# First loads reordered, two units sharing a norm's high parts, the reciprocal ahead of the splits, and two more buffers for the last weights

## The reference

```python
h = rmsnorm(x, g[0]);  y = even_mixer(h)      # gated heads (HGRN2) and retention, h @ w_in, then @ w_out
x = x + rmsnorm(y, g[1])
h = rmsnorm(x, g[2]);  x = x + rmsnorm(square(relu(h @ w1)) @ w2, g[3])      # MLP 0
h = rmsnorm(x, g[0']); x = x + rmsnorm(odd_mixer(h), g[1'])                  # mLSTM heads, causal conv
h = rmsnorm(x, g[2']); x = x + rmsnorm(square(relu(h @ w1')) @ w2', g[3'])   # MLP 1
h = rmsnorm(x, n) * (1 + scale) + shift       # shift, scale, gate = silu(c) @ w_ada + b_ada
y_attn = (attention(h) * silu(g_attn)) @ w_o_attn;  y_conv = (short_conv(h) * silu(g_conv)) @ w_o_conv
x = x + gate * ((sigmoid(m_attn) * y_attn + sigmoid(m_conv) * y_conv) @ w_out)
return rmsnorm(x, final_g)
```

## Time and profile before

| | us |
|---|---|
| median of 3 executions | 1048.25 (1048.1 to 1050.12) |
| profiled execution | 1048.74 |
| its span | 1046.7 |
| TensorE busy | 998.1 (95%) |
| VectorE busy | 669.5 (64%) |
| ScalarE busy | 510.9 (49%) |
| mean granted clock of TensorE | 0.982 of full |

### The profile page before, as it was taken

The page is one execution under the profiler, slowest core; times in us unless marked ns, Lnnn a source line. Parts: engine busy times, 40 slices in busy tenths (PEclk is TensorE's granted clock), DMA queues, the critical chain, the costliest instruction groups (busy, mean ns, idle before and its releaser), DMA issues.

```text
span 1046.7 us, 16188 instructions
## 1 busy us (share of the span) xinstructions
PE 998.1 (95%) x6914; PEld 935.1 (89%) x6914; DVE 669.5 (64%) x825; ACT 510.9 (49%) x567; POOL 25.6 (2%) x22
## 2 busy tenths in 40 slices
PE   4998999899999999989999999997999999999986
PEld 3998999699999988989789999996999999989975
DVE  5679859767666757484767666657434677645453
ACT  6543564664435347354554344356344555445432
POOL 0000002100000000000200000000000000001000
PEclk8999999999999998988999999999999999999999
DMA  9743422747677673433437776792765544466511
GB/s 316 233 159 121 144 99 82 260 143 261 226 239 238 222 228 121 121 121 121 138 130 241 256 241 202 241 244 79 242 200 166 165 155 162 162 201 210 193 41 41
DMA packets 141291, 187.48 MB, mean 179 GB/s; under 512 B 5315, under 2 KB 125604, under 8 KB 141220
## 3 DMA queue, kind: packets, MB, share of 16 engines
q1 hardware_dynamic: 141204, 186.44, 54.8%
q10 hardware_dynamic: 16, 0.01, 0.0%
HBM read 185.37 MB, written 1.06 MB: 178 GB/s over the span
## 4 chain that ended last, share of the span: by engine, by line
PE 49%; DVE 3%; ACT 2%; issue 1%; DVEq 0%; ACTq 0%
PE bank L504 49%; DVE wl L909 1%; ACT wh L1436 1%; DVE arena L915 0%; DVE arena L909 0%; DVE arena L912 0%; ACT hh L1429 0%; PE bank L643 0%; PE bank L794 0%; DVE hl L909 0%; DVE x L915 0%; ACT arena L1429 0%; ACT L1429 0%; DVE yl L909 0%; ACT yh L1502 0%
## 5 line engine op out<-in xcount | busy, mean ns | idle before, releaser
L909 DVE TENSOR_TENSOR wl<-raw,wh 128x2048 fp32r<-128x2048 f32 x158 | 360.5, 2290 | 233.8 <-ACT wh L1436 156.5
L504 PE MATMUL bank<-hh,wh 128*128 128x256 f32 x1312 | 373.8, 289 | 5.3 <-DVE wl L909 5.3
L504 PE MATMUL bank<-hh,wl 128*128 128x256 f32 x1312 | 368.1, 285 | 0.0
L504 PE MATMUL bank<-hl,wh 128*128 128x256 f32 x1312 | 363.4, 284 | 1.3 <-DVE hl L909 1.2
L1436 ACT CAST wh<-raw 128x2048 fp32r<-128x2048 f32 x158 | 298.5, 1906 | 119.1 <-PE bank L504 116.3
L504 PEld LDWEIGHTS bank<-hh,wh 128*128 128x128 f32 x1312 | 251.8, 194 | 6.0 <-issue 5.7
L504 PEld LDWEIGHTS bank<-hh,wl 128*128 128x128 f32 x1312 | 251.7, 194 | 0.0
L504 PEld LDWEIGHTS bank<-hl,wh 128*128 128x128 f32 x1312 | 248.9, 193 | 2.3 <-DVE hl L909 2.1
L504 PE MATMUL bank<-wh,yh 128*128 128x512 f32 x432 | 169.0, 391 | 7.9 <-DVE yl L909 3.1
L504 PE MATMUL bank<-wl,yh 128*128 128x512 f32 x432 | 168.3, 390 | 0.0
L504 PE MATMUL bank<-wh,yl 128*128 128x512 f32 x432 | 168.1, 389 | 0.0
(11 more groups left out here) (160 smaller groups left out, 726.9 us busy)
## 6 DMA issues: line engine op xcount, KB each, us to landing
raw<-in_mlp_w SPq DMA_DIRECT2D x64, 1024.0 KB, 5.5
raw<-in_w_in SPq DMA_DIRECT2D x40, 1024.0 KB, 5.1
raw<-in_ev_w_in SPq DMA_DIRECT2D x20, 1024.0 KB, 5.5
raw<-in_w_ada SPq DMA_DIRECT2D x12, 1024.0 KB, 5.2
raw<-in_od_w_in SPq DMA_DIRECT2D x12, 1024.0 KB, 5.3
raw<-in_ev_w_out SPq DMA_DIRECT2D x6, 1024.0 KB, 4.8
raw<-in_od_w_out SPq DMA_DIRECT2D x4, 1024.0 KB, 5.0
raw<-in_w_o_conv SPq DMA_DIRECT2D x4, 1024.0 KB, 5.2
```

Source lines behind the costliest of these rows:

```text
L504: return eng.matmul(o, l, r, start=start, stop=stop, skip_group_check=True)
L909: return eng.tensor_tensor(o, x, y, op)
```

## The change

- SP: identity between the halves of x, `rows1` behind them, then unit 0; the other three small loads behind unit 0. TensorE transposes `rows1` and then x at once; the rest of the small work follows (`small_columns` on VectorE stands behind the split of unit 0).
- `a_first`: at the start, high products first, then `hl`, and the products with `wl` last. At norms 1 to 4 it takes two units: the `hh` products of both, then (norms 1 to 3) the spread, then the `hl` products of both.
- ScalarE's `x_root`: the squares of the first row block at the end of `postnorm`, the second's and the root behind `hh` and ahead of the splits; VectorE's reciprocal likewise ahead of its splits (in norm 2 behind two of eight `work` blocks, which free the bank that the spread writes).
- The last two units have their own `wh` and `wl`: one in `hh` and `hl`, one over `work` and over `bias` (`part`, `wait_home`). All four units of out6 are split at units NU - 7 and NU - 6, in the order NU - 4, NU - 2, NU - 1, NU - 3.
- The first turn of merged stands ahead of the last quarter of out5, the second behind the first quarter of out6, and `b_last` takes all four units in each quarter.
- The last norm: half 0 is multiplied by the gain on VectorE while the root is made, and by the reciprocal on ScalarE; half 1 stays on VectorE. ScalarE issues the store of block 1, half 0.

```diff
+OWN = (NU - 2, NU - 1)
...
-    if u in ENDS:
+    if u in (NU - 7, NU - 6):
+        return [NU - 4, NU - 2] if u == NU - 7 else [NU - 1, NU - 3]
+    if u in ENDS or u > NU - 6:
...
+SPLIT_OF, LOW_OF, _low = {}, {}, {"dve": 0, "ada": 0}
+for _u in range(-AHEAD, NU):
+    for _s in splits_at(_u):
+        _by = "ada" if UNITS[_s][0] == "C" else "dve"
+        _low[_by] += 1
+        LOW_OF[_s] = (_by, _low[_by])
+        if _by == "dve":
+            SPLIT_OF[_s] = len(SPLIT_OF)
+assert sorted(LOW_OF) == list(range(NU))
...
+        wl_end = place("wl_end", (P, UELEMS), F32R, cursor[0] - 8192)
...
+        wh_end = place("wh_end", (P, UELEMS), F32R, masks_at - 7168)
...
+        def part(t, u):
...
+            if u in OWN and t is not raw:
+                if u == OWN[0]:
+                    return (hh if t is wh else hl)[:, :, :].rearrange("p k t -> p (k t)")
+                return (wh_end if t is wh else wl_end)[:, :]
+            return t[:, u % RING, :]
...
+            return part(t, u).rearrange("p (k c) -> p k c", k=2 if kind == "B" else KT)
...
+        def wait_home(eng, u):
...
+            if u in OWN:
+                wait_used(eng, last_of("ma"))
+                eng.wait_ge(S["lg"], ATT_HEADS)
+                eng.wait_ge(S["p"], ATT_HEADS)
+                eng.wait_ge(S["pt"], ATT_HEADS)
+            elif u >= RING:
+                wait_used(eng, u - RING)
...
+            eng.dma_start(ident[:, :], a["tbl"][:, T_IDENT:T_IDENT + P]).then_inc(S["d_rows"], 16)
...
+            eng.dma_start(rows1[0:ROWS1, :], a["rows1"]).then_inc(S["d_rows"], 16)
...
+                    eng.dma_start(rows2[0:ROWS2, :], a["rows2"]).then_inc(S["d_small"], 16)
+                    eng.dma_start(rel_in, a["rel_bias"]).then_inc(S["d_small"], 16)
+                    eng.dma_start(onehot, a["tbl"][0:32, T_ONEHOT:T_ONEHOT + SEQ]).then_inc(S["d_small"], 16)
...
+                for half, done in enumerate((S["fin_act"], S["fin_dve"])):
+                    if (t, half) != (1, 0):
+                        eng.wait_ge(done, t + 1)
+                        eng.dma_start(out[t * P:(t + 1) * P, half_of(half)], fin_t[:, t, half_of(half)]).then_inc(S["d_out"], 16)
...
+                units = (u,) if norm == 0 else (u, u + 1)
...
+                def both(v, w, h, k, first=False, last=False):
+                    o = bank(v)
...
+                        if FORM[UNITS[v][3]] == "F":
...
-                wait_low(eng, u)
...
+                def low_products(v):
+                    for k in range(KT):
+                        eng.wait_ge(S["hl"], KT * norm + k + 1)
+                        m = both(v, slot(wh, v, "A"), hl, k, last=norm != 0 and k == KT - 1)
+                    return m
...
+                for v in units:
+                    if v != u:
+                        eng.wait_ge(S["hi"], SPLIT_OF[v] + 1)
+                        wait_evac(eng, A_UNITS[A_OF[v] - 2])
+                    if norm != 0:
+                        wait_low(eng, v)
+                    for k in range(KT):
+                        eng.wait_ge(S["hh"], KT * norm + k + 1)
+                        both(v, slot(wh, v, "A"), hh, k, first=k == 0)
+                        if norm != 0:
+                            both(v, slot(wl, v, "A"), hh, k)
+                if norm == 0:
+                    low_products(u)
+                    wait_low(eng, u)
+                    for k in range(KT):
+                        m = both(u, slot(wl, u, "A"), hh, k, last=k == KT - 1)
+                    m.then_inc(S["used"], 1)
+                    return
+                if norm in LATE:
+                    x_spread(norm)
+                for v in units:
+                    low_products(v).then_inc(S["used"], 1)
...
+                        if PHASE[UNITS[u][3]] == 5 and (t, half) == (1, 1):
+                            merged_turn(0)
...
-                    merged_turn(t)
...
-                    for pair in range(2 if t == 0 else 1):
-                        units = range(first + 2 * pair, first + 2 * pair + 2) if t == 0 else range(first, NU)
-                        if t == 0:
...
+                    for half in range(2):
+                        for u in range(first, NU):
+                            if (t, half) == (0, 0):
...
-                            if (t == 1 or pair == 1) and (t, half) != (1, 1):
...
+                            m = b_part(u, t, half, u == first, u == NU - 1)
+                            if (t, half) == (1, 1):
+                                m.then_inc(S["used"], 1)
+                        if (t, half) != (1, 1):
+                            m.then_inc(S["acc"], 1)
+                        if (t, half) == (0, 0):
+                            merged_turn(1)
...
-            eng.wait_ge(S["d_small"], 16 * 5)
-            eng.transpose(PS[2][:, 0:ROWS1], rows1[0:ROWS1, :], ident[0:ROWS1, 0:ROWS1])
-            eng.transpose(PS[2][:, P:P + ROWS2], rows2[0:ROWS2, :], ident[0:ROWS2, 0:ROWS2])
+            eng.wait_ge(S["d_rows"], 32)
+            eng.transpose(PS[2][:, 0:ROWS1], rows1[0:ROWS1, :], ident[0:ROWS1, 0:ROWS1]).then_inc(S["colsT"], 1)
+            x_turn(0)
+            eng.wait_ge(S["d_small"], 16 * 3)
+            eng.transpose(PS[3][:, SEQ:SEQ + ROWS2], rows2[0:ROWS2, :], ident[0:ROWS2, 0:ROWS2])
...
-            x_turn(0)
...
-                if kind == "A":
+                if PRENORM.get(u - 1, 0) != 0:
+                    pass
+                elif kind == "A":
...
-                        a_forward(u, {at("mog", 3): ml_spread,
-                                      at("up0", 1): lambda: x_spread(1), at("mv", 1): lambda: x_spread(2),
-                                      at("up1", 1): lambda: x_spread(3)}.get(u))
+                        a_forward(u, {at("mog", 3): ml_spread}.get(u))
...
+                wait_home(eng, u)
+                tt(part(wl, u), part(raw, u), part(wh, u).bitcast(F32),
...
+                    if n == 0:
+                        eng.wait_ge(S["colsT"], 1)
+                        tensor(col1[:, :], PS[2][:, 0:ROWS1]).then_inc(S["cols"], 1)
+                        eng.wait_ge(S["cols"], 1)
...
-                if n == 2:
...
+                for part, blocks in enumerate(((2, 3), (0, 1, 4, 5, 6, 7)) if n == 2 else ()):
+                    for k in blocks:
...
+                    if part == 0:
+                        x_root(n)
+                if n in (1, 3):
+                    x_root(n)
...
+            def small_columns():
+                eng.wait_ge(S["colsT"], 2)
+                tensor(col2[:, :], PS[3][:, SEQ:SEQ + ROWS2]).then_inc(S["cols"], 1)
+                tensor(u_row[:, P - 1:P - 1 + SEQ], PS[3][0:ATT_HEADS, 0:SEQ]).then_inc(S["u"], 1)
+                link(tt(lbs[:, 2, :], low[0], low[1], ALU.max))
+                link(tt(lbs[:, 2, :], lbs[:, 2, :], low[2], ALU.max))
+                for r in range(3):
+                    tt(lb[:, r, :], low[r], lbs[:, 2, :], ALU.subtract).then_inc(S["low"], 1)
...
+                if u == -AHEAD:
+                    small_columns()
...
-                    x_root(PRENORM[u])
...
+                tt(fin_p[:, t, half_of(0)], x[:, t, half_of(0)], fin_gain[:, half_of(0)], ALU.mult).then_inc(S["fin_g"], 1)
...
+                eng.reciprocal(rs[:, 8 + t:9 + t], sd[:, 10 + t:11 + t]).then_inc(S["fin_rs"], 1)
+                eng.wait_ge(S["fin_rs"], t + 1)
+                c = half_of(1)
+                stt(fin_t[:, t, c], x[:, t, c], rs[:, 8 + t:9 + t], fin_gain[:, c], ALU.mult,
+                    ALU.mult).then_inc(S["fin_dve"], 1)
...
+                wait_home(eng, u)
+                eng.copy(part(wh, u), part(raw, u)).then_inc(S["hi"], 1)
...
+                squares(junk_x[:, 1, :], x[:, 1, :], 5, S["x_ssq"])
...
+                    eng.wait_ge(S["cols"], 1)
...
+                if n in LATE:
+                    x_root(n)
...
+                if n + 1 in LATE:
+                    eng.wait_ge(S["x_n"], 4 * n + 2)
+                    squares(junk_x[:, 0, :], x[:, 0, :], 4, S["x_ssq"])
...
-                if PRENORM.get(u) in LATE:
-                    x_root(PRENORM[u])
...
+                eng.wait_ge(S["fin_g"], t + 1)
+                eng.wait_ge(S["fin_rs"], t + 1)
+                act(fin_t[:, t, half_of(0)], fin_p[:, t, half_of(0)], ACT.Copy,
+                    scale=rs[:, 8 + t:9 + t]).then_inc(S["fin_act"], 1)
+                if t == 1:
+                    eng.wait_ge(S["fin_act"], 2)
+                    eng.dma_start(out[P:2 * P, half_of(0)], fin_t[:, 1, half_of(0)]).then_inc(S["d_out"], 16)
```

More of the change, by code:

```diff
@@ L167 @@
 A_OF = {}
-SPLIT_OF = {}
 for _u, _it in enumerate(UNITS):
@@ L171 @@
         A_OF[_u] = len(A_OF)
[L172 to L178, removed]
 EVAC = {"hf": "act", "hq": "act", "hi": "act", "rq": "dve", "rk": "dve", "rv": "act", "hgate": "act",
@@ L280, in build @@
             "u asc lg mxn gle aexp p tr pt aout aout_v mcm merged acc_free4 acc_free5 d_gain "
-            "fin_x fin_ssq fin_b fin_sd fin_rs fin_o"
```

(29 more changed lines are left out.)

40 lines of the change are left out of this document (1 added, 39 removed).

## The result

| | before | after |
|---|---|---|
| median of executions | 1048.9 us (1048.1 to 1050.12, 4) | **1032.52 us** (1031.74 to 1033.57, 4) |
| profiled execution, its span | 1048.74, 1046.7 | 1031.78, 1029.9 |
| mean granted clock of TensorE | 0.982 | 0.987 |

The ratio is 0.985, 95% interval 0.9832 to 0.9868. The forecast was 1032.8. Its sum came out; of its terms, those of the start and the end were too large and the others too small.

A forecast was written before the change was run, and what follows sets the result against it. TensorE, busy 95% of the 1046.7 us span, bounds the kernel. Terms 6.9 + 0.15 + 0.85 + 0.15 + 2.1 + 5.0 + 0.5 = 15.65 off 1048.74 give 1033.1, from the median 1032.6; forecast 1032.8, range 1029.5 to 1038.

The forecast's parts named there:

- Start: Start of kernel: earlier scaling of x, earlier unit 0 weights and reordered products gain 6.9 us, bounds 5.8 and 7.6.
- Rival E: Start: loads reordered but first weights land no earlier, 10.4; 0.9 us less gain, 1033.7; chance 0.62 together with the forecast.
- The low clock: Start: TensorE's clock stays low for the first 4.8 us of unit 0's products, counted from 12.1.
- Its survival: Gated heads after the start: VectorE has 3.3 us of slack, less about 1.3, so the start's gain survives whole.
- Norms 1 and 3: Pairing units behind norms 1 and 3 gains 0.15 us each, bank wait covered by 0.6; bounds 0 less 1.0, and 0.2.
- Norm 2: Spread at norm 2 no longer waits 0.80 us for reciprocals: gain 0.85, bounds 0 and 0.9.
- rival C: Low-clock stretches fall elsewhere: 1033.9 to 1038.4, or luckily 1.5 to 3 us less, 1030; chance 0.15.
- Norm 4: Norm 4: with 64 high products first, no `hl` is waited for; gain 2.1 us, bounds 1.2 and 2.2.
- Last phase: Around out5 and out6: waits for `yl` twice and `wl` once removed; gain 5.0 us, bounds 3.9 and 5.1.
- rival B: Around out5 and out6: casts wait for a load, merge is late, 1.5 to 3 us return; 1034.5 to 1036; chance 0.07.
- End: Last norm: sharing final products with ScalarE and issuing its store there gains 0.5 us, bounds 0.2 and 0.75.
- D: Clock stays low from the early start through the first units, whole gain gone or worse, 1049 to 1053; chance 0.04.

The follow-up runs named there:

- The unaltered kernel's second trace: The changed kernel with no edit, run again beside later runs on one chip: this trace 1030.93 us; median 1032.6 us.
- the warmed one: Changed kernel plus seven products of ones on TensorE ahead of its first transpose, nothing else altered: one execution, 2496.26 us.
- the other warmed run: Changed kernel plus seven products of ones on TensorE, small columns behind unit 1's split and the relative bias store behind the third cast: 1032.75 us.

## Why the prediction was right

**Start: mechanism right, mis-sized by 0.9** (6.9 forecast, 5.97). The term that was off is the landing of unit 0's weights. The prediction put it at 9.5, between 8.8 and 10.4; it was 10.70, beyond the upper bound, though issued 1.7 us earlier. Rival E is what happened, with 0.3 more; x came later too. The estimate took for granted that an earlier issue wins something of its 1.7 us; in twelve traces of the new order it won nothing, though by 10.7 us as many bytes had moved as before by 10.4 (2.9 MB). Why stays open. From there the sums held: `hl` done and `wl` begun 5.9 us behind the landing (6.0 forecast), the subtraction and columns 3.3, `wl` of unit 1 2.2, the first products behind it at 22.28. The low clock, forecast for 4.8 us of work, lasted until 19.3, 6.2 us into the products, and cost nothing: TensorE was through with unit 0 at 21.8, before unit 1's `wl`. The unaltered kernel's second trace bears that out: there the clock rose at 16.4, and unit 1 still started 11.58 behind the landing.

**Its survival: right.** The decays' three waits kept their lengths, and the undone start gave back 6.0 at norm 1.

**Norms 1 and 3:** 0.31 and 0.32 for 0.15 each, and no wait for a bank came back at either. **Norm 2:** the wait of 0.80 went, as forecast; most of the rest is a low stretch of 3.4 us that before's trace has at 397 and this trace has not. The changed kernel run again does have one there, and takes 17.33 us from norm 2's turn to the gate products against 18.38 before, a gain of 1.05. So 1.5 of the 16.8 was luck of the profiled execution, a share of what rival C had named for the good side, and it hid the two terms that came out too large. Without it the parts add to 15.25 for 15.65. **Norm 4:** 2.38 for 2.1; the two units take 11.6 us (712.51 to 724.10), where one took 8.05 and the other 5.76, so 2.2, the upper bound; 0.1 each came in the turn ahead and behind.

**Last phase:** 5.35 measured between landmarks and 5.36 by undoing it, for 5.0 (bounds 3.9 to 5.1). No wait returned, so rival B is out: the fourth cast of the units ended soon enough, at 991.3, the merge at 997.06, and the second half of the turn didn't wait for it.

**End: wrong, 0.0 for 0.5.** This step of the prediction failed: it counted when the last store is issued. What ends the span is the transfer of both stores, which begins with the first and is bound by its bytes.

**Clock.** The record of the granted clock has 40.8 us of low clock before and 29.7 after; 6.8 of the difference are the start's, 3.4 norm 2's, 0.8 the end's. The start's part is no gain. The record after begins only at 19.3 (below), and up to there TensorE did 6.2 us of products at the low pace, against 4.8 before. Rows 4 also read otherwise than the prediction says: the last transpose before ended at 15.06, and the clock fell at 18.3, 3.2 us later and not 5. D did not come: unit 1's products stand 0.12 apart from the first on.

## What to carry to other kernels

When a product is a sum of parts that get ready one after another, do the parts in the order in which they get ready, and the last one's making lies under the others; that gave 4.8 of 16.8 us here. Don't book an earlier issue of a load as an earlier landing: here 1.7 us of it gave nothing, and the reason wasn't found. And before a last operation is shared between two engines, look whether the transfers behind it are what ends, and whether a small operation that moves has a waiter in another engine's queue, ahead of something large.

## What was not expected of the hardware

The granted clock reads 1.00 in the changed kernel from 8 to 19.5 us (windows, PEclk behind the busy times), while the 16 `hh` products took 3.75 us, 0.23 each, and 16 products in the high clock 2.07. The record of the clock in that trace begins at 19.3 us, with the rise; before that there is no entry, and full speed is shown. At the start the pace of the products has to be read, not this column.

```profile
8.00:13.00 5.00, 4.62 (x18) 2.85 (x16) 1.11 (x3) 2.78 (x6) 0.00 (x0) 1.00 1.06 347
13.00:19.50 6.50, 6.38 (x30) 6.41 (x31) 6.02 (x13) 4.32 (x8) 0.00 (x0) 1.00 1.11 351
```

Apart from the start and the end, low stretches are 3.4, 6.8 or 10.2 us long in all thirteen traces that have a record of the clock, and one of 3.4 that TensorE works through costs about 1.6 us. The first four executions of the changed kernel lie near two levels 1.6 apart (1031.74 and 1031.78; 1033.26 and 1033.57), which would fit one such stretch; the four later ones, 1030.93 to 1034.85, don't show the levels. An edit of under 1 us can't be told by the total here, only by landmarks, and those of the start have to be counted from the landing of unit 0, which moves by 0.5 us between traces of one order.

Single executions among the last ones took 4213 us (the kernel before), 2927 (the changed one) and 2496 (the warmed one). The trace of the last shows TensorE busy all the time, each group of 16 products in 4.98 us, where the high clock gives 2.07 and the low clock about 3.4. It was so from the start: the seven products of ones took 8.60 us, and 4.75 in the other warmed run. This trace has no entry on the clock at all, so the granted clock of 1.00 that its views print says nothing. What held it back the trace does not show.

```profile
15.85 4.97 PE L530 MATMUL bank<-hh,wh 128*128 128x256 f32 x16
20.65 4.99 PE L530 MATMUL bank<-hl,wh 128*128 128x256 f32 x16
25.36 4.98 PE L530 MATMUL bank<-hh,wl 128*128 128x256 f32 x16
```
